# Projections split in two f32r terms: one 512-column matmul for the high weights, one of 256 for the low weights, and the two halves of the bank summed on VectorE

## The chip, the cores and the metric

One Trainium2 chip, one of its NeuronCores. The metric is the device time of one launch in microseconds, as a median over runs. One launch computes three layers of a small transformer-like stack for 256 tokens of width 2048.

## What is computed

The reference runs three layers one after the other in fp32. In outline (`@` is a matrix product over 2048 features unless said otherwise):

```
# layer A: modulated norm, sparse attention and a pooled branch, then experts
ada  = silu(c) @ w_ada + b_ada                      # six vectors of 2048
h    = rmsnorm(x) * (1 + sc1) + sh1
q, k, v, qi, ki, wi, p = split(h @ w_in)
mix  = concat(attention_topk(q, k, v, qi, ki, wi), pool(p))
x    = x + gt1 * (mix @ w_out)
x    = x + gt2 * experts(rmsnorm(x) * (1 + sc2) + sh2)   # top 2 of 32, SwiGLU
# layer B: gated linear recurrence and sliding-window attention
z    = rmsnorm(x) @ l0_w_in                         # lx, lg, bq, bk, bv, bs
x    = x + concat(rg_lru(lx) * silu(lg), window_attention(bq, bk, bv) * silu(bs)) @ l0_w_out
# layer C: latent attention and differential attention
z    = rmsnorm(x) @ l1_w_in                         # cq, ckv, kr, mg, dq, dk, dv, dg
q, kv = rmsnorm(cq) @ w_uq, rmsnorm(ckv) @ w_ukv
x    = x + concat(mla(q, kv, kr) * silu(mg), diff_attention(dq, dk, dv) * silu(dg)) @ l1_w_out
out  = rmsnorm(x)
```

## The kernel before

Activations lie transposed: 128 features on the partitions, 256 tokens along the free dimension, 16 chunks for 2048 features. A **projection** computes one chunk of 128 output features for all 256 tokens. Its weights are 16 blocks of 128 x 128, one for each chunk `kk` of input features, and arrive from HBM in two halves of eight blocks (512 KB each, `land`).

**Split operands.** TensorE's one-pass type f32r has fewer bits than fp32, so both operands are split. ScalarE copies a half of the weights to `WH` in f32r (step `hi`, L1370), and VectorE subtracts that from the original to get the rest, `WL` (step `lo`, L1654). The activations are split in the same way to `HH` and `HL` (steps `hh`/`hl`, `mh`/`ml`, `ch`/`cl`). Three matmuls for each block, all in one bank (`product`, L992), make the product: WH by HH, WL by HH, WH by HL. The weights are the stationary operand and 256 tokens the moving one, so each of the three loads 128 x 128 weights and streams 256 columns. 2552 blocks go this way. The value projections v, bv, dv and vm are **wide**: there the activations are stationary (L989).

**Stages.** Layer A's projections run with the streaming of `w_ada` between them (L1042), then come its attention jobs, the output projection `wo`, and a router. The experts follow (L1181 to L1235), a loop that streams 12 MB of weights for each tile of tokens. Then layer B (projections bk to lg, eight attention jobs, four groups of the recurrence, `wb`) and layer C (cq to mg, attention jobs `d`, the up-projections qn, qr, kn and vm with jobs `m`, then `wc`).

**Order of the work.** `order_a` and `order_bc` write out by hand, for each of PE, ACT and DVE, the list of steps that the engine runs in that order. A step waits for the steps it needs through one semaphore for each engine, and each engine also waits for its own step before. `Order.proj` adds a projection: the PE's `part` and `proj`, the evacuation `evac` on ACT, and a `load` (that is `hi` on ACT and `lo` on DVE) after each half, four halves ahead of their use. Later steps of older projections or jobs (norm, rotation, softmax) are added by `tick`.

**Banks.** Projections, the index products and every second gate product of the recurrence (`lgate`, L1148) take turns in two PSUM banks, `acc0` and `acc1`. In `bank_of` the PE waits until the step two before in that list has left its bank; before the change that is ACT's `evac`. For k, q, cq and ckv, `evac` makes a copy and a square. For wo, wb and wc it makes a copy `tm`, and DVE's step `res` adds that to the residual `X` (L1783).

## Time and profile before

| what | value |
|---|---|
| median of 3 runs | 2473.24 us (2471.9 to 2474.04) |
| span of the profiled execution | 2472.8 us |
| PE busy | 2121.0 us (86%) |
| DVE busy | 1214.8 us (49%) |
| ACT busy | 898.2 us (36%) |
| granted TensorE clock, mean | 0.938 of full speed |

The span is what the profile shows of one execution, from the first to the last instruction; the times of the runs are taken without the profiler. Names of tiles are the program's, L numbers are lines of the kernel before. PEld is TensorE's loading of weights, which overlaps its matmuls.

### The profile page before, as it was taken

The page shows a single profiled execution, that of the slowest core. Times are in us where ns is not written, and L with a number is a line of the kernel's source. Part 1 is how long each engine was busy: PE and PEld are TensorE (multiplying, and loading weights), DVE is VectorE, ACT ScalarE, POOL GpSimd, SP SyncE. Part 2 cuts the span into 40 slices and gives each one's busy share as a digit, 9 for nine tenths or more (in the row PEclk, how much of TensorE's full clock was granted, in tenths as well). Part 3 has the DMA queues.
Part 4 walks back from the last instruction along what each step waited for, and adds up shares of the span by engine and source line. Part 5 has one row for each costly group of instructions (what it writes and reads, how often), then busy time and mean ns, then how long its engine had stood idle before and what let it go on. Part 6 is the DMA issues. An engine that isn't in the chain of part 4 may idle for free.

```text
span 2472.8 us, 38254 instructions
## 1 busy us (share of the span) xinstructions
PE 2121.0 (86%) x14524; PEld 1408.1 (57%) x14524; DVE 1214.8 (49%) x2202; ACT 898.2 (36%) x1382; POOL 0.2 (0%) x4
## 2 busy tenths in 40 slices
PE   5699998986888788878887888799989799998987
PEld 1178776772222222222222222599889799997887
DVE  1254686445433333333333433646875554478555
ACT  1143344442211122211122121546865444465543
POOL 0000000000000000000000000000000000000000
PEclk7799999997999989999999999899999899998999
DMA  8979776766999999999999998365345355543442
GB/s 320 383 278 315 263 264 247 264 222 254 422 422 422 422 422 422 422 422 422 422 422 422 422 422 349 110 202 163 120 136 182 128 171 185 181 146 102 132 129 100
DMA packets 135046, 695.44 MB, mean 281 GB/s; under 512 B 14992, under 2 KB 15120, under 8 KB 85264
## 3 DMA queue, kind: packets, MB, share of 16 engines
q1 hardware_dynamic: 134928, 693.81, 73.5%
q8 instruction: 81, 1.33, 0.2%
q14 instruction: 37, 0.30, 0.0%
HBM read 691.66 MB, written 2.10 MB: 281 GB/s over the span
## 4 chain that ended last, share of the span: by engine, by line
PE 48%; DMA 37%; DVE 8%; ACT 4%; issue 2%; SPq 1%; DVEq 0%; ACTq 0%
DMA ring<-in_w 33%; PE acc L992 33%; DMA land<-in_stream_a 4%; PE acc L989 3%; PE psS L1218 3%; PE psO L1042 2%; DVE WL L1654 2%; ACT WH L1370 1%; PE psM L1073 1%; SPq L872 1%; DVE HL L1664 0%; ACT SB L1440 0%; PE psT L938 0%; PE psM L1206 0%; PE acc L1108 0%
## 5 line engine op out<-in xcount | busy, mean ns | idle before, releaser
L992 PE MATMUL acc<-HH,WH 128*128 128x256 f32 x2552 | 752.5, 295 | 47.4 <-DVE HL L1664 15.7
L992 PE MATMUL acc<-HH,WL 128*128 128x256 f32 x2552 | 728.9, 286 | 0.0
L992 PE MATMUL acc<-HL,WH 128*128 128x256 f32 x2552 | 728.5, 285 | 0.0
L1654 DVE TENSOR_TENSOR WL<-land,WH 128x1024 fp32r<-128x1024 f32 (+1 forms) x350 | 425.7, 1216 | 423.8 <-ACT WH L1370 419.7
L992 PEld LDWEIGHTS acc<-HH,WH 128*128 128x128 f32 x2552 | 495.9, 194 | 92.1 <-issue 16.2
L992 PEld LDWEIGHTS acc<-HH,WL 128*128 128x128 f32 x2552 | 497.0, 195 | 3.3 <-issue 2.2
L992 PEld LDWEIGHTS acc<-HL,WH 128*128 128x128 f32 x2552 | 496.4, 195 | 0.0
L1370 ACT ACTIVATE WH<-land 128x1024 fp32r<-128x1024 f32 (+1 forms) x350 | 367.9, 1051 | 252.9 <-PE acc L992 199.2
L1218 PE MATMUL psS<-ring,low 128*32 128x512 f32 x2048 | 282.8, 666 | 148.2 <-DMA ring<-in_w 126.2
L1218 PEld LDWEIGHTS psS<-ring,low 128*32 128x32 f32 x2048 | 53.8, 113 | 340.3 <-DMA ring<-in_w 251.7
L2037 DVE TENSOR_REDUCE SB<-psT 128x128 f32<-128x512 f32 x32 | 22.1, 692 | 389.5 <-PE psT L1228 389.5
L1206 PE MATMUL psM<-low 128*128 128x512 f32 x264 | 146.1, 635 | 23.3 <-DVE low L2028 21.2
L1518 ACT ACTIVATE low<-psO 128x512 f32<-128x512 f32 x32 | 19.1, 597 | 340.5 <-PE psO L1235 340.5
L1042 PE MATMUL psO<-land,high_a 128*32 128x512 f32 x672 | 103.8, 698 | 39.7 <-DMA land<-in_stream_a 37.5
L1206 PE MATMUL acc<-low 128*128 128x512 f32 x264 | 135.7, 596 | 0.0
L1512 ACT ACTIVATE low<-psS 128x512 f32<-128x512 f32 x64 | 38.2, 597 | 226.3 <-PE psS L1218 225.9
L1235 PE MATMUL psO<-ring,SB 128*32 128x512 f32 x1024 | 116.5, 595 | 0.0
L2028 DVE TENSOR_TENSOR low<-psM,low 128x512 f32<-128x512 f32 x132 | 91.1, 690 | 44.4 <-PE psM L1206 44.3
L2049 DVE TENSOR_SCALAR low<-low,cst 128x256 f32<-128x256 f32 x128 | 36.5, 349 | 140.3 <-ACT low L1522 140.3
L2028 DVE TENSOR_TENSOR low<-acc,low 128x512 f32<-128x512 f32 x132 | 90.9, 689 | 17.4 <-PE acc L1206 17.4
L1206 PEld LDWEIGHTS psM<-low 128*128 128x128 f32 x264 | 39.7, 189 | 100.8 <-DVE low L2028 98.2
L1181 PE MATMUL acc<-low,SB 128*32 128x512 f32 x528 | 82.7, 757 | 15.4 <-DVE SB L2006 15.4
(326 smaller groups left out, 1998.4 us busy)
## 6 DMA issues: line engine op xcount, KB each, us to landing
ring<-in_w SPq DMA_DIRECT2D x384, 1024.0 KB, 24.1
land<-in_stream_a SPq DMA_DIRECT2D x284, 512.0 KB, 7.3
land<-in_stream_bc SPq DMA_DIRECT2D x246, 512.0 KB, 4.0
land<-in_stream_bc SPq DMA_DIRECT2D x12, 384.0 KB, 3.3
X<-in_xT SPq DMA_DIRECT2D x1, 2048.0 KB, 16.3
out<-low SPq DMA_DIRECT2D x4, 512.0 KB, 2.7
cst<-in_const SPq DMA_DIRECT2D x1, 1538.0 KB, 12.4
low<-in_w_pool SPq DMA_DIRECT2D x1, 1024.0 KB, 5.2
```

The costliest lines, as they stand in the source:

```text
L989: mm = pe.matmul(bank[:, S * tt:S * tt + S], h[:, rows[kk], P * tt:P * tt + P], w[:, kk, :], start=(z == 0 and i == 0 and tt == 0), stop=s ...
L992: mm = pe.matmul(bank[:, 0:S], w[:, kk, :], h[:, rows[kk], :], start=(z == 0 and i == 0), stop=stop)
L1042: mm = pe.matmul(bank[CAP * c:CAP * c + CAP, :], cB[:, 4 * q + c, :], w[c // 2][:, c % 2, :], start=(q == 0), stop=(q == 3), tile_position ...
L1181: mm = pe.matmul(bG[CAP * n:CAP * n + CAP, :], SG[:, tt, :], H2[:, tt, 512 * n:512 * n + 512], start=(tt == 0), stop=(tt == NT - 1), tile_ ...
L1206: pe.matmul(ybank[m % 2], OE[:, P * c:P * c + P], SJ[:, 2 * half:2 * half + 2, :], start=True, stop=True).then_inc(moe["y_full"], 1)
L1218: mm = pe.matmul(bH[s // 4][CAP * c:CAP * c + CAP, :], XG[:, k % 4, k // 4, :], ring[:, s, 512 * c:512 * c + 512], start=(s % 4 == 0), sto ...
L1235: mm = pe.matmul(bW2[CAP * c:CAP * c + CAP, :], AT[:, s - 8, :], ring[:, s, 512 * c:512 * c + 512], start=(s == 8), stop=(s == 11), tile_p ...
L1370: ins = act.activation(WH[:, q % PARTS, 0:n], land[k][:, p % LAND[k], 0:n], ACT.Copy)
L1512: act.activation(HS[:, b, :], bankS[b], ACT.Copy).then_inc(moe["h_copied"], 1)
L1654: ins = dve.tensor_tensor(WL[:, q % PARTS, 0:n], land[k][:, p % LAND[k], 0:n], WH[:, q % PARTS, 0:n].bitcast(F32), ALU.subtract)
L2028: dve.tensor_tensor(y, src, y, ALU.add).then_inc(moe["y_added"], 1)
L2049: ins = dve.tensor_scalar(SJ[:, c, :], ST, K("group", c, 1), None, ALU.mult)
```

## The change

For projections that are not wide, WH by HH and WH by HL become one matmul of 512 columns. For that, HH and HL are the two halves of one tensor `HHL`; the first half of the bank takes WH by HH, the second WH by HL, and WL by HH is added to the first half as before. The two halves of the bank then have to be summed: a new DVE step `sum` adds the second half to what ACT's `evac` has copied of the first, and `bank_of` waits for that step. For wo, wb and wc there is no ACT copy any more: DVE's `res` adds each half of the bank to X, one after the other. The squares of k, q, cq and ckv become an ACT step of their own, `square`, which waits for `sum` and reads SBUF.

```diff
+SUMMED = ("k", "q", "qi", "ki", "wi", "p", "wo", "bk", "bq", "bs", "lx", "lg", "wb", "cq", "ckv", "kr", "dk", "dq", "dg", "mg",
+          "qn", "qr", "kn", "wc")
+RESIDUAL = ("wo", "wb", "wc")
...
         self.acc.append(("proj", x))
-        self.add("act", "evac", x)
+        if x[0] not in RESIDUAL:
+            self.add("act", "evac", x)
+            if x[0] in SUMMED:
+                self.add("dve", "sum", x)
+        if x[0] in ("k", "q", "cq", "ckv"):
+            self.add("act", "square", x)
...
-        HH = inside("HH", [P, KD, S], F32R, 8 * PARTS)
-        HL = inside("HL", [P, KD, S], F32R, 8 * PARTS + KD)
+        HHL = inside("HHL", [P, 2, KD, S], F32R, 8 * PARTS)
+        HH, HL = HHL[:, 0, :, :], HHL[:, 1, :, :]
...
-                terms = [(a, b, c, kk) for kk in range(len(rows)) for a, b, c in ((wh, HH, 0), (wl, HH, 1), (wh, HL, 2))]
+                terms = [(a, b, c, kk) for kk in range(len(rows)) for a, b, c in
+                         (((wh, HH, 0), (wl, HH, 1), (wh, HL, 2)) if wide else ((wh, HHL, 0), (wl, HH, 1)))]
...
+                        elif term == 0:
+                            mm = pe.matmul(bank.rearrange("p (a s) -> p a s", a=2), w[:, kk, :], HHL[:, :, rows[kk], :],
+                                           start=(z == 0 and i == 0), stop=False)
                         else:
-                            mm = pe.matmul(bank[:, 0:S], w[:, kk, :], h[:, rows[kk], :], start=(z == 0 and i == 0), stop=stop)
+                            mm = pe.matmul(bank[:, 0:S], w[:, kk, :], h[:, rows[kk], :], start=False, stop=stop)
...
-                        needs(k, "act", o, "evac", prev[1] if prev[0] == "proj" else prev)
-                    return acc[n % 2]
+                        if prev[0] == "proj":
+                            needs(k, evac_of(prev[1])[0], o, *evac_of(prev[1])[1:])
+                        else:
+                            needs(k, "act", o, "evac", prev)
+                    return acc[n % 2][:, :]
...
+                def add_other(x):
+
+                    other = acc[o.acc.index(("proj", x)) % 2][:, S:2 * S]
+                    needs("act", "evac", x)
...
+                    return dve.tensor_tensor(z, other, z, ALU.add)
...
-                            needs("act", "evac", step[1])
-                            tm = W((aTM if k == 0 else dTM) + n % 2)[:, 0, :]
-                            ins = dve.tensor_tensor(X[:, n, :], X[:, n, :], tm, ALU.add)
+                            needs("pe", "proj", step[1])
+                            bank, x = acc[o.acc.index(("proj", step[1])) % 2], X[:, n, :]
+                            for h in range(2):
+                                a = bank[:, S * h:S * h + S]
+                                if name == "wo":
+                                    ins = dve.scalar_tensor_tensor(out=x, in0=a, scalar=gt1[:, n:n + 1], in1=x, op0=ALU.mult, op1=ALU.add)
+                                else:
+                                    ins = dve.tensor_tensor(x, a, x, ALU.add)
+                                if h == 0:
+                                    then(ins)
```

**PE, layer B, around a gate product.** The end of a projection, an attention job's products (L946, L910), the two gate products (L1148) and the start of the next projection. Before:

```order
4109 L992 MATMUL acc<-HH,WL 128x256
4110 L992 MATMUL acc<-HL,WH 128x256
4111 L946 MATMUL psO<-PTS,low 128x512 [waits dve_done1,act_done1]
4112 L910 MATMUL psS<-low 128x2x128 [waits dve_done1]
4116 L1148 MATMUL acc<-low 128x256 [waits act_done1,dve_done1]
4117 L1148 MATMUL acc<-low 128x256
4118 L992 MATMUL acc<-HH,WH 128x256 [waits dve_done1,act_done1]
4119 L992 MATMUL acc<-HH,WL 128x256
4120 L992 MATMUL acc<-HL,WH 128x256
```

The same place in the changed kernel:

```order
2906 L1010 MATMUL acc<-HHL,WH 128x512
2907 L1013 MATMUL acc<-HHL,WL 128x256
2908 L963 MATMUL psO<-PTS,low 128x512 [waits dve_done1,act_done1]
2909 L927 MATMUL psS<-low 128x2x128 [waits dve_done1]
2913 L1172 MATMUL acc<-low 128x256 [waits dve_done1]
2914 L1172 MATMUL acc<-low 128x256
2915 L1010 MATMUL acc<-HHL,WH 128x512 [waits dve_done1]
2916 L1013 MATMUL acc<-HHL,WL 128x256
```

Three matmuls for a block have become two, and the first matmul of the next projection no longer waits for ACT but for DVE alone.

**DVE, at the same place.** `low<-psO` is a job's output, `SB<-psS` its softmax, `high_bc` and `low<-high_bc` the recurrence, `WL` the low parts of the weights. Before:

```order
690 L1654 TENSOR_TENSOR WL<-land_54,WH 128x1024 [waits act_done1,dve_done1] x2
691 L1942 TENSOR_TENSOR high_bc<-high_bc 128x256 [waits act_done1,dve_done1]
692 L1943 SCALAR_TENSOR_TENSOR low<-high_bc 128x256 [waits dve_link]
695 L1654 TENSOR_TENSOR WL<-land_54,WH 128x1024 [waits act_done1,dve_done1] x2
696 L1620 TENSOR_TENSOR low<-psO,low 64x2x128 [waits pe_done1,dve_done1]
```

Now:

```order
811 L1697 TENSOR_TENSOR WL<-land_53,WH 128x1024 [waits act_done1,dve_done1]
812 L1666 TENSOR_TENSOR low<-acc,low 128x256 [waits act_done1,dve_done1]
813 L1697 TENSOR_TENSOR WL<-land_53,WH 128x1024 [waits act_done1,dve_done1]
814 L1990 TENSOR_TENSOR high_bc<-high_bc 128x256 [waits act_done1,dve_done1]
815 L1991 SCALAR_TENSOR_TENSOR low<-high_bc 128x256 [waits dve_link]
818 L1697 TENSOR_TENSOR WL<-land_53,WH 128x1024 [waits act_done1,dve_done1]
819 L1666 TENSOR_TENSOR low<-acc,low 128x256 [waits act_done1,dve_done1]
820 L1697 TENSOR_TENSOR WL<-land_53,WH 128x1024 [waits act_done1,dve_done1]
821 L1644 TENSOR_TENSOR low<-psO,low 64x2x128 [waits pe_done1,dve_done1]
```

Between the two `lo` steps that stood in a pair there is now the sum of a projection (L1666), behind whatever DVE has still to do.

## Rows read from the trace of the kernel before

**Rows 1.** The page: busy time, share of the span, instructions.

```profile
PE 2121.0 (86%) x14524; PEld 1408.1 (57%) x14524; DVE 1214.8 (49%) x2202; ACT 898.2 (36%) x1382; POOL 0.2 (0%) x4
```

**Rows 2.** The page: the chain that ended last, by engine and by line.

```profile
PE 48%; DMA 37%; DVE 8%; ACT 4%; issue 2%; SPq 1%; DVEq 0%; ACTq 0%
DMA ring<-in_w 33%; PE acc L992 33%; DMA land<-in_stream_a 4%; PE acc L989 3%; PE psS L1218 3%; PE psO L1042 2%; DVE WL L1654 2%; ACT WH L1370 1%; PE psM L1073 1%; SPq L872 1%; DVE HL L1664 0%; ACT SB L1440 0%; PE psT L938 0%; PE psM L1206 0%; PE acc L1108 0%
```

**Rows 3.** Stretches of the span: engines' busy us, granted clock, DMA share, GB/s.

```profile
core 0: us, PE busy (x) PEld busy (x) DVE busy (x) ACT busy (x) POOL busy (x), PEclk, DMA share, GB/s
186.00:248.00 62.00, 62.00 (x488) 50.88 (x487) 28.33 (x43) 20.35 (x25) 0.00 (x0) 1.00 0.91 316
2030.00:2090.00 60.00, 60.00 (x503) 60.00 (x502) 25.65 (x22) 26.08 (x31) 0.00 (x0) 1.00 0.57 181
1720.00:1850.00 130.00, 121.66 (x876) 111.00 (x876) 106.77 (x183) 98.70 (x160) 0.00 (x0) 0.99 0.40 131
```

**Rows 4.** The chain by line in 310 to 440, 1720 to 1850, 2190 to 2370 us.

```profile
by line: PE acc L992 25.3%; PE acc L1108 8.0%; DVE WL L1654 7.6%; DMA land<-in_stream_a 5.4%; PE psM L1042 5.4%; DVE high_a L1744 5.3%; issue 4.8%; DVE small L1743 4.6%; PE psS L905 2.9%; DVE low L1705 2.7%; ACT WH L1370 2.5%; PE psT L938 1
by line: PE acc L992 48.9%; DVE WL L1654 6.7%; issue 5.6%; ACT WH L1370 4.1%; PE psS L910 3.3%; PE psO L946 3.3%; ACT SB L1440 2.4%; PE psT L938 2.4%; PE psM L1148 2.0%; PE acc L1148 2.0%; DVE SB L1607 2.0%; ACT L1440 2.0%; DVE HL L1676 1.9
by line: PE acc L992 39.7%; ACT WH L1370 6.3%; DVE WL L1654 5.2%; ACT SB L1440 4.9%; PE acc L989 4.8%; PE psO L951 4.5%; issue 4.2%; PE psS L915 3.3%; ACT HH L1396 2.4%; PE psT L938 2.2%; ACT low L1401 2.1%; DVE high_bc L1966 1.9%; PE psM L
```

**Rows 5.** Chain pieces: start us, length us, what.

```profile
1717.47 5.75 PE acc L992 x48
1723.22 1.72 PE psO L946 x4
1734.13 0.44 PE psT L938 x4
2314.26 0.22 PE psS L922 x2
```

**Rows 6.** Timeline of PE at the upper clock: start us, length us, instruction.

```profile
2020.14 0.28 PE L992 MATMUL acc<-HH,WL 128*128 128x256 f32 x1
2020.14 0.19 PEld L992 LDWEIGHTS acc<-HL,WH 128*128 128x128 f32 x1
2020.26 0.28 PE L992 MATMUL acc<-HL,WH 128*128 128x256 f32 x1
```

**Rows 7.** Timeline of PE at the lower clock, from 427.34 us.

```profile
427.69 0.42 PE L992 MATMUL acc<-HH,WL 128*128 128x256 f32 x1
...
429.83 0.41 PE L992 MATMUL acc<-HL,WH 128*128 128x256 f32 x1
```

**Rows 8.** Groups: shapes and count, busy us, mean ns of one, idle before and what ended it.

```profile
L938 PEld LDWEIGHTS psT<-cst,SB 128*128 128x128 f32 x120 | 13.5, 143 | 15.2 <-DVE SB L1607 6.7 <-DVE SB L1602 6.0 <-issue 1.7
L922 PEld LDWEIGHTS psS<-low 128*128 128x128 f32 x32 | 5.3, 191 | 0.3
L1716 DVE TENSOR_TENSOR low<-psT,cst 128x256 f32<-128x256 f32 x19 | 8.1, 425 | 1.5 <-PE psT L1092 0.9
L1783 DVE TENSOR_TENSOR X<-X,high_bc 128x256 f32<-128x256 f32 x32 | 13.6, 426 | 28.6 <-ACT high_bc L1311 28.5
L1311 ACT ACTIVATE high_bc<-acc 128x256 f32<-128x256 f32 x32 | 12.4, 387 | 60.2 <-PE acc L992 57.3 <-issue 3.0
```

**Rows 9.** Timeline around a gate product at 1775 us.

```profile
1775.94 1.03 PE L1148 MATMUL acc<-low 128*128 128x256 f32 x4
1776.09 0.38 ACT L1329 ACTIVATE low<-acc 128x256 f32<-128x256 f32 x1
1776.62 0.47 PE L992 MATMUL acc<-HH,WH 128*128 128x256 f32 x1
1777.17 0.69 DVE L1943 TENSOR_TENSOR_SCAN low<-high_bc 128x256 f32<-128x256 f32 x1
1777.90 2.49 DVE L1654 TENSOR_TENSOR WL<-land,WH 128x1024 fp32r<-128x1024 f32 x2
```

**Rows 10.** Timeline around the next gate product, at 1799 us.

```profile
1799.05 0.38 ACT L1329 ACTIVATE low<-acc 128x256 f32<-128x256 f32 x1 [1.46 <-PE acc L992]
1800.76 0.47 PE L992 MATMUL acc<-HH,WH 128*128 128x256 f32 x1
1802.49 2.48 DVE L1654 TENSOR_TENSOR WL<-land,WH 128x1024 fp32r<-128x1024 f32 x2
```

**Rows 11.** Timeline of DVE in the up-projections of layer C.

```profile
2301.35 3.35 DVE L1966 RECIPROCAL high_bc<-high_bc 128x512 f32<-128x512 f32 x1
```

More of the change, by code:

```diff
@@ L124, in constants, with evac_of @@
     return t
+SUMMED = ("k", "q", "qi", "ki", "wi", "p", "wo", "bk", "bq", "bs", "lx", "lg", "wb", "cq", "ckv", "kr", "dk", "dq", "dg", "mg",
+          "qn", "qr", "kn", "wc")
+RESIDUAL = ("wo", "wb", "wc")
+def evac_of(x):
+    if x[0] in RESIDUAL:
+        return "dve", "res", x
+    return ("dve", "sum", x) if x[0] in SUMMED else ("act", "evac", x)
 LAGS = {"a": (1, 2, 3, 4), "b": (1, 2, 3, 4), "d": (1, 2, 3, 4), "m": (1, 3, 5, 6)}
@@ L917, in attention @@
                     else:
-                        needs(k, "act", o, "evac", ("kn", 4 * j[1] + 3))
+                        needs(k, "dve", o, "sum", ("kn", 4 * j[1] + 3))
                         needs(k, "dve", o, "rot", ("qr", 3))
@@ L1054, in run @@
                         misc_free(step)
-                        needs(k, "act", o, "evac", ("wi", 0))
+                        needs(k, "dve", o, "sum", ("wi", 0))
                         for tt in range(NT):
@@ L1071, in run @@
                         else:
-                            needs(k, "act", o, "sq" if x[0] == "moe" else "evac", x)
+                            needs(k, "act", o, "sq" if x[0] == "moe" else "square", x)
                         mm = pe.matmul(psM[:, 0:S], ones[:, :], sq, start=(x in FIRST_SS), stop=(x[1] == LAST.get(x[0], KD - 1)))
@@ L1076, in run @@
                         misc_free(step)
-                        needs(k, "act", o, "evac", x)
+                        needs(k, "act", o, "square", x)
                         mm = pe.matmul(psM[:, 0:S], ones[:, :], W(aSQ + nr.index(x) % 2)[:, 0, :], start=True, stop=True)
@@ L1090, in run @@
                         else:
-                            needs(k, "act", o, "evac", x)
+                            needs(k, "dve", o, "sum", x)
                         mm = pe.matmul((psM if n is None else bankT[0])[:, 0:S], K(rot_of(x)), rot_chunk(x), start=True, stop=True)
@@ L1275, in evac @@
                     if name in ("k", "q"):
-                        i = nr.index(x)
-                        if i >= 2:
-                            needs("pe", "nrm", nr[i - 2])
-                        act.activation(rot_chunk(x), a, ACT.Copy)
-                        return act.activation(W(aSQ + i % 2)[:, 0, :], a, ACT.Square)
+                        return act.activation(rot_chunk(x), a, ACT.Copy)
                     if name in ("qi", "ki", "qr"):
@@ L1341, in evac @@
                     if name in ("cq", "ckv"):
-                        if n >= 2:
-                            needs("pe", "ss", (name, n - 2))
-                        act.activation(W((cCQ if name == "cq" else cCKV) + n)[:, 0, :], a, ACT.Copy)
-                        return act.activation(W(dSQ + n % 2)[:, 0, :], a, ACT.Square)
+                        return act.activation(W((cCQ if name == "cq" else cCKV) + n)[:, 0, :], a, ACT.Copy)
                     if name in ("dk", "dq"):
@@ L1357, in run @@
                         ins = evac(step[1])
+                    elif what == "square":
+                        x = step[1]
+                        name, n = x
+                        needs("dve", "sum", x)
+                        if name in ("k", "q"):
+                            i = nr.index(x)
+                            if i >= 2:
+                                needs("pe", "nrm", nr[i - 2])
+                            ins = act.activation(W(aSQ + i % 2)[:, 0, :], rot_chunk(x), ACT.Square)
+                        else:
+                            if n >= 2:
+                                needs("pe", "ss", (name, n - 2))
+                            ins = act.activation(W(dSQ + n % 2)[:, 0, :], W((cCQ if name == "cq" else cCKV) + n)[:, 0, :], ACT.Square)
                     elif what == "silu_c":
@@ L1399, in run @@
                         _, name, n, size = step
+                        needs("dve", "sum", (name, n + size - 1))
                         z = W(MIX + n + (8 if name in ("bs", "dg") else 0), size)
@@ L1625, in attention_out @@
                     return dve.tensor_tensor(mix, psO[:, :, :], mix, ALU.mult)
+                def add_other(x):
+                    other = acc[o.acc.index(("proj", x)) % 2][:, S:2 * S]
+                    needs("act", "evac", x)
+                    name, n = x
+                    if name == "bk":
+                        z = W(bK + 2 * n, 2)
+                        dve.tensor_tensor(z[0:64, 0, :], other[0:64, :], z[0:64, 0, :], ALU.add)
+                        return dve.tensor_tensor(z[64:128, 1, :], other[64:128, :], z[64:128, 1, :], ALU.add)
+                    at = {"wi": aWI, "p": aPR, "bq": bQ, "lg": MIX, "mg": MIX, "bs": MIX + 8, "dg": MIX + 8, "cq": cCQ, "ckv": cCKV,
+                          "dk": cDK, "dq": cDQ, "qn": cQN, "kn": cKN}
+                    if name in ("k", "q", "qi", "ki", "qr", "kr"):
+                        z = rot_chunk(x)
+                    else:
+                        z = W(bLX + n % 2 if name == "lx" else at[name] + n)[:, 0, :]
+                    return dve.tensor_tensor(z, other, z, ALU.add)
                 def rms(n, width):
@@ L1634, in run @@
                         dve.wait_ge(done[k]["dve"], count)
-                    if what == "setup":
+                    if what == "sum":
+                        ins = add_other(step[1])
+                    elif what == "setup":
                         dve.memset(ones[:, :], 1.0)
@@ L1751, in run @@
                         p = W(aPR + 2 * g, 2)
-                        needs("act", "evac", ("p", 2 * g + 1))
                         a, b = W(aPS, 2), W(aPS + 2, 2)
@@ L1915, in run @@
                         n = step[1]
-                        needs("act", "evac", ("lx", n))
                         x, y = W(bLX + n % 2)[:, 0, :], W(bY + n)[:, 0, :]
@@ L1949, in run @@
                         p = step[1]
-                        needs("act", "evac", ("dk", 2 * p + 1))
                         if p:
```

8 lines of the change are left out of this document (1 added, 7 removed).

## The prediction

> **What bounds the kernel now.** Read the busy shares first: TensorE (PE) is busy 86% of the span, VectorE (DVE) 49%, ScalarE (ACT) 36% [rows 1]. A share says nothing of single stages, so the chain that ended last comes next [rows 2]: a third of it is the DMA of expert weights, which this change does not touch, and another third, 33% of 2472.8 us or 816 us, is line L992, the three-matmul product that it rewrites. DVE has 8% of the chain, ACT 4%. So the product is on the path for most of its time, and outside the experts a faster product shortens the kernel if the next limit is not close behind.
>
> How close it is shows in the stretches [rows 3]. At 2030 to 2090 us PE is busy without a gap, and DVE only 25.65 of 60 us: there a gain on PE is a gain. At 1720 to 1850 us DVE is busy 106.77 and ACT 98.70 of 130 us. The chain of that stretch, and of 310 to 440 us and 2190 to 2370 us, changes often between PE, DVE and ACT, with L992 at 48.9%, 25.3% and 39.7% [rows 4]. There DVE work is on the path too. DMA has room: its share is 0.91 at 316 GB/s in one of the densest stretches of layer A, and 0.57 in layer C [rows 3].
>
> **What a matmul of the product costs.** In a steady run 48 of them take 5.75 us [rows 5], 119.8 ns each; the timeline shows the same spacing of 0.12 us, and each load of weights starting with the matmul before it [rows 6]. The clock there is the upper level of 2.4 GHz (granted 1.00, [rows 3]), so 256 columns at one a cycle are 106.7 ns, and 13.1 ns are something else. What? Three rows help. At the lower level, 1.2 GHz, ten matmuls take 2.14 us [rows 7], 214 ns each against 213.3 for 256 columns: the rest is hidden. The fp32 products, two cycles a column in each record, take 430 ns for 512 columns and 110 ns for 128 [rows 5], against 426.7 and 106.7: a rest of 3 ns, and this holds for a short load of 143 ns (L938) and a full one of 191 ns (L922) alike [rows 8]. So a full load alone fits into about 110 ns. The 13 ns appear only where columns stream at one a cycle with a load beside them.
>
> **The change on PE.** For each block it removes one load of weights and one matmul, and makes another twice as wide. Now: 3 x 119.8 = 359.4 ns. After: one of 256, taken at 119.8 ns, and one of 512, which no row shows at one column a cycle. Its bounds: from below 213.3 + 3 = 216 ns, if the rest belongs to a load that hinders the stream (the load covers less than half of 512 columns); from above 2 x 119.8 = 239.6 ns, if the stream itself runs at 0.468 ns a column. Between them lies a fixed cost for each matmul, 213.3 + 13.1 = 226.4 ns. I take 222 ns, midway between 216 and 226.4 with the fp32 rows in mind: they speak for a small fixed part. That is 341.6 ns a block, a saving of **17.8 ns**; the fixed cost alone would give 13.2 ns.
>
> The Trainium skill (TensorE: Matmul & The Clock Gate, Back-to-back issue gap) gives for an isolated matmul at the upper clock N/2.4 + 2.5 ns: 109.2 ns for 256 columns and 215.8 for 512. By that rule a block would go from 327.5 to 325.0 ns and the change would save 2.5 ns. The trace shows 119.8 instead of 109.2 for this product, so the rule does not describe it, and the sum goes by the rows.
>
> **How many blocks count.** 816 us of chain are 2270 blocks of 359.4 ns, of 2552. In the three mixed stretches L992 has 0.253 x 130 + 0.489 x 130 + 0.397 x 180 = 168 us of chain [rows 4], or 467 blocks. A second chain on DVE and ACT runs close beside there, so I count half of them. 2270 - 234 = 2036 blocks by 17.8 ns are **36.2 us gained**.
>
> **The change on DVE and ACT.** 125 projections get a `sum`: a 256-column DVE operation with one input in PSUM, as L1716, 425 ns [rows 8]; 127 instructions, since bk needs two, 54 us. Each residual step becomes two such operations instead of one of 426 ns on SBUF (L1783): 48 more, 20 us. ACT loses the 48 copies of wo, wb and wc, 387 ns each (L1311), 19 us. In the PE-bound stretches DVE's idle time hides all of this: a projection there takes 5.5 us, its two `lo` steps 2.5, its sum 0.43. In the mixed stretches there are some 55 projections (about 10, 17 and 28); 55 x 0.44 = 24 us of new DVE work, and half of it falls where DVE is on the path: **12 us lost**.
>
> **The wait that the change adds.** The PE may write a bank again only after DVE's `sum`, where ACT's copy was enough. Between two projections on end there are 5.5 us for that, and nothing waits. But a gate product takes the other bank, so the next projection needs at once the bank of the last one. At 1776 us ACT had copied it by 1776.47 and the PE went on at 1776.62, while the DVE pair of `lo` steps that now has the sum between them ran from 1777.90 to 1780.39 [rows 9]: the sum would end at 1779.6, 3.0 us after the PE's start. At 1799 us the same comes to 1804.2 against 1800.76, 3.4 us [rows 10]. The first two gate products come earlier or find DVE free. The up-projections kn are short (four blocks, under 1.5 us), and one can stand behind the reciprocal of 3.35 us [rows 11]. Together 6.4 + up to 3.4; the stretches that follow are partly DVE's anyway, so I take **8 us**. ACT's new `square` waits for DVE in the middle of its queue, with `hi` behind it: half a microsecond for 20 projections, which the four halves split ahead cover, and at the stage ends, where the last residual chain stays as long (a PSUM add for an ACT copy), about **1 us**. The wide projections keep their form.
>
> **Sum**: -36.2 + 12 + 8 + 1 = -15 us, on the profiled span of 2472.8 us: 2458 us. The median of the runs, 2473.24, lies 0.4 us from that span, so this serves as the forecast for the median too. About 0.2%, 4.9 us, is what a measurement of this kernel can tell from no change.
>
> **Rivals.** *The load is the whole rest.* Then 512 columns cost 216 ns and the narrow matmul, with a load beside fewer streaming columns, about 113: 329 ns a block, 30 ns saved, 61 us over 2036 blocks; less 21 us, 2433 us. For it: the fp32 rows with their rest of 3 ns, and the lower clock without one. Against it: the narrow matmul keeps a full load beside it.
>
> *The stream is the limit.* If one-pass f32r data cannot be read faster than 0.468 ns a column, two halves in one matmul cost 239.6 ns, PE gains nothing, and the sums and bank waits remain: +21 us at most, some of them hidden in PE's slack, 2490 us. For it: a full-rate stream of 4-byte elements is the one thing that sets this product apart from the fp32 rows. Against it: nothing in the trace needs it. It decides from 229 ns for the wide matmul on: below a saving of 21 us / 2036 = 10.3 ns a block the kernel is not faster. The skill's rule above would end here too: 2.5 ns a block are 5 us, 2489 us.
>
> *DVE becomes the bound.* If in the mixed stretches each of the 55 projections pays its sum and a wait behind half a `lo` pair, 0.44 + 0.6 us, 57 us stand in place of 20; with the gain of 36 us, 2494 us. For it: DVE is busy 82% of 1720 to 1850 us. Against it: for most of layers A and C it has over half its time free.
>
> **Chances.** The forecast with its near cases (a saving of 13 to 20 ns a block, 2450 to 2467 us) 0.45; the load 0.25; the stream 0.20; DVE 0.10. Nearly all of the first two is faster by over 0.2%, the upper edge of the forecast is not; in the last two a part may end within 0.2%: faster 0.64, same 0.11, slower 0.25. The range leaves out the outer part of each rival: 2428 to 2488 us.
>
> **What would show it.** Right: wide matmuls spaced 216 to 227 ns at full clock, blocks of about 342 ns, PE busy through 2030 to 2090 us with fewer microseconds for each projection, DVE near 1290 us, and PE waits on the new DVE sum of some 3 us at two gate products. Wrong: wide matmuls at 240 ns; PE waits on sums at every projection of a mixed stretch; or waits on DMA in layer A, which the 0.91 leaves little room for.

## The result, and the profile after

The changed kernel is slower, by less than one per cent. Its median is 2490.52 us (2486.77 to 2491.46, 4 runs) against 2473.64 (2471.9 to 2476.71, 4 runs) of the kernel before: a ratio of 1.007, 95% interval 1.0056 to 1.0084, or 14 to 21 us. The profiled execution has a span of 2488.6 us against 2472.8.

The first section and the chain of the page of the changed kernel answer to [rows 1] and [rows 2]. L1010 is the 512-column matmul, L1013 the one of 256, L1007 the value projections that kept their form:

```profile
PE 2111.5 (85%) x11972; PEld 1272.3 (51%) x11972; DVE 1290.2 (52%) x2377; ACT 881.5 (35%) x1334; POOL 0.2 (0%) x4
PE 45%; DMA 37%; DVE 10%; ACT 5%; issue 2%; SPq 1%; DVEq 0%; ACTq 0%
```

TensorE issues 2552 matmuls and loads fewer, and the product has 31% of the chain (L1010 21%, L1013 10%) after 33%. VectorE has 75.4 us more work (74 in the forecast), and its share of the chain went from 8 to 10%.

The timeline of TensorE in a dense piece of layer C (start us, length us, instruction) stands beside [rows 6]:

```profile
2050.12 0.40 PE L1010 MATMUL acc<-HHL,WH 128*128 128x512 f32 x1
2050.35 0.28 PE L1013 MATMUL acc<-HHL,WL 128*128 128x256 f32 x1
2050.47 0.40 PE L1010 MATMUL acc<-HHL,WH 128*128 128x512 f32 x1
2050.71 0.28 PE L1013 MATMUL acc<-HHL,WL 128*128 128x256 f32 x1
2050.83 0.40 PE L1010 MATMUL acc<-HHL,WH 128*128 128x512 f32 x1
```

A block, wide and narrow, takes 0.35 to 0.36 us. In 2030 to 2090 us, where TensorE never stops, the starts of the narrow matmuls lie 346, 356 and 358 ns apart in turn, 353.4 ns in the mean of 170; in the kernel before all 167 blocks of that stretch take 360.0 ns. The change saves **6.6 ns** a block where the forecast had 17.8. Over the undisturbed blocks of 1850 to 2090 us the saving is 7.5 ns: a wide matmul takes 235.7 ns from start to start (572 of them) and the narrow one 116.6 (573), 352.3 together, against 359.9.

Stretches of the span, as in [rows 3]:

```profile
2030.00:2090.00 60.00, 60.00 (x342) 52.05 (x341) 31.85 (x36) 26.34 (x32) 0.00 (x0) 1.00 0.56 187
1720.00:1850.00 130.00, 110.34 (x548) 88.75 (x546) 105.91 (x188) 91.65 (x144) 0.00 (x0) 0.93 0.36 118
```

In the first TensorE is busy without a gap, as it was. In the second it is busy 110.34 us of 130 after 121.66, and its granted clock is 0.93 after 0.99: it waits more, and part of its work runs slower. For what it waits, the view of the waits says (what waits, for what, us in total, times, longest), for 1742 to 1845 us and then for 2290 to 2385 us:

```profile
PE acc L1010 <- DVE low L1666: 10.6, 3, 5.2
...
PE acc L1010 <- DVE low L1666: 5.1, 2, 4.2
```

L1666 is the new `sum`. In the kernel before the longest waits of these stretches were for the split activations, and no wait of the product on a copy out of the bank was among the listed ones:

```profile
PE acc L992 <- DVE HL L1676: 5.9, 2, 3.5
...
PE acc L992 <- DVE HL L1676: 3.8, 2, 2.2
```

A third new wait stands in 226 to 348 us, where the q projections run; there TensorE is held by ScalarE's copy of the index product (L1317, high_a), and ScalarE by the sum, before the square (L1376):

```profile
PE acc L1010 <- ACT high_a L1317: 5.2, 5, 1.4
ACT high_a L1376 <- DVE low L1666: 4.3, 4, 1.7
```

The program has the same 354 halves of projections in both kernels, so the start of each can be set against the start of the same one before. The changed kernel stands 1.1 us behind at the end of the experts (1591 us), gains down to 1.4 us ahead by 1742 us, loses 15.1 us from there to 1842 us, gains 4.1 by 2298 us, loses 8.9 by 2382 us. This reading is used for all kernels below.

The three stretches that lose are shown here over the same work in both kernels, first of the kernel before, then of the changed one, with the columns of [rows 3]:

```profile
226.60:348.10 121.50, 114.21 (x819) 89.04 (x818) 81.35 (x147) 46.37 (x73) 0.00 (x0) 0.99 0.78 273
1742.00:1842.10 100.10, 91.76 (x663) 83.80 (x661) 85.20 (x147) 79.26 (x122) 0.00 (x0) 0.98 0.39 127
2298.00:2382.30 84.30, 75.47 (x586) 72.88 (x585) 49.83 (x65) 46.95 (x85) 0.00 (x0) 0.98 0.35 113
...
221.80:349.60 127.80, 115.90 (x626) 79.87 (x625) 85.90 (x159) 47.37 (x73) 0.00 (x0) 0.96 0.74 260
1740.70:1855.90 115.20, 95.54 (x469) 77.56 (x468) 90.47 (x159) 78.88 (x121) 0.00 (x0) 0.91 0.34 112
2307.70:2400.90 93.20, 79.57 (x468) 69.97 (x467) 56.50 (x82) 46.20 (x83) 0.00 (x0) 0.91 0.30 102
```

They take 30.3 us more. TensorE stands idle for 20.7 of these us, and is busy for 9.6 us more although it has less to do, because more of its work falls into time at the lower of its two clock levels (1.2 and 2.4 GHz): a share of 0.5 is the lower level, so 121.5 x 0.01, 100.1 x 0.02 and 84.3 x 0.02, taken twice, give some 10 us of such time before, and the shares below them some 48 us now. The 501 blocks of these stretches should have saved 3.3 us, so the lower clock costs about 13 us, an estimate from these rows.

### The profile page after: what moved, and what is told of

Same layout as the page of the kernel before. It is cut to its first block, busy times and chain, and to the rows that moved or that the text cites. A ratio compares the mean times of both kernels' runs of the same rounds, so it can differ in the third digit from the quotient of the medians.

```text
span 2488.6 us, 33366 instructions
## 1 busy us (share of the span) xinstructions
PE 2111.5 (85%) x11972; PEld 1272.3 (51%) x11972; DVE 1290.2 (52%) x2377; ACT 881.5 (35%) x1334; POOL 0.2 (0%) x4
## 4 chain that ended last, share of the span: by engine, by line
PE 45%; DMA 37%; DVE 10%; ACT 5%; issue 2%; SPq 1%; DVEq 0%; ACTq 0%
DMA ring<-in_w 33%; PE acc L1010 21%; PE acc L1013 10%; DMA land<-in_stream_a 4%; PE acc L1007 3%; PE psS L1242 3%; DVE WL L1697 2%; PE psO L1066 2%; ACT WH L1393 2%; SPq L889 1%; PE psM L1097 1%; ACT SB L1464 1%; DVE HHL L1707 0%; PE psM L1230 0%; PE psO L968 0%
## 5 line engine op out<-in xcount | busy, mean ns | idle before, releaser
L1010 PE MATMUL acc<-HHL,WH 128*128 128x512 f32 x2552 | 952.1, 414 | 66.4 <-DVE HHL L1707 16.5
L1013 PE MATMUL acc<-HHL,WL 128*128 128x256 f32 x2552 | 727.3, 285 | 0.0
L1010 PEld LDWEIGHTS acc<-HHL,WH 128*128 128x128 f32 x2552 | 492.2, 193 | 230.2 <-DVE HHL L1707 22.6
L1013 PEld LDWEIGHTS acc<-HHL,WL 128*128 128x128 f32 x2552 | 495.8, 194 | 3.4 <-issue 2.4
L1666 DVE TENSOR_TENSOR low<-acc,low 128x256 f32<-128x256 f32 x115 | 48.8, 424 | 68.8 <-ACT low L1357 13.7
```

Source lines behind the costliest of these rows:

```text
L1010: mm = pe.matmul(bank.rearrange("p (a s) -> p a s", a=2), w[:, kk, :], HHL[:, :, rows[kk], :], start=(z == 0 and i == 0), stop=False)
L1013: mm = pe.matmul(bank[:, 0:S], w[:, kk, :], h[:, rows[kk], :], start=False, stop=stop)
```

## The experiments

Each ratio below is to runs of the kernel before that were taken together with the experiment; their medians lie between 2471.1 and 2474.2 us. The expectations are in us without such a correction, so a miss of one or two us says nothing.

### The two halves of the change, one at a time

`e1_three_mm` keeps sums, waits and both halves of the bank and takes the wide matmul away:

```
-  (((wh, HH, 0), (wl, HH, 1), (wh, HL, 2)) if wide else ((wh, HHL, 0), (wl, HH, 1)))
+  ((wh, HH, 0), (wl, HH, 1), (wh, HL, 2))
...
+  half = S if term == 2 else 0
+  mm = pe.matmul(bank[:, half:half + S], w[:, kk, :], h[:, rows[kk], :], ...)
```

> The sums, their waits and the use of both halves of the bank stay; the 512-column matmul is split back into two of 256, high by high into the first half and high by low into the second. Against the kernel before this carries the sums and waits alone, against the changed kernel it lacks the wide matmul alone. Theory A (the two parts add up: the wide matmul saves some 5 ns a block over 2036 to 2552 blocks, 10 to 13 us, and the sums with their waits cost 27 to 30): 2500 to 2503 us. Rival B (the sums cost only where PE comes to a bank too early, so that a slower PE hardly waits): 2485 to 2492, about the changed kernel's time. Rival C (the wide matmul itself costs time, the sums are nearly free): 2473 to 2478.

Measured: 2508.21 us, ratio to before 1.0154 (1.0136 to 1.0171): sums and waits cost 34 to 42 us. That is above theory A's 2500 to 2503 us, and further from both rivals.

`e2_no_sums` is the kernel before with the wide matmul alone; its output lacks the product of high weights and low activations:

```
-  HH = inside("HH", [P, KD, S], F32R, 8 * PARTS)
-  HL = inside("HL", [P, KD, S], F32R, 8 * PARTS + KD)
+  HHL = inside("HHL", [P, 2, KD, S], F32R, 8 * PARTS)
...
+  mm = pe.matmul(bank[:, :].rearrange("p (a s) -> p a s", a=2), w[:, kk, :], HHL[:, :, rows[kk], :], ...)
```

> The kernel before with the wide matmul alone: the second half of the bank (high weights by low activations) is computed and never added, so this product is left out of the output; steps, waits and copies are those of the kernel before. Theory A (a block goes from 359 to some 354 ns, nothing else): 2460 to 2464 us. Rival D (the forecast's step was right in itself, 341.6 ns a block, and its gain was eaten by waits): 2435 to 2445. Rival C (the wide matmul costs time): over 2476.

Measured: 2456.05 us, ratio 0.9938 (0.992 to 0.9956): 11 to 20 us faster, somewhat more than theory A's 2460 to 2464 us. The interval holds the 2270 blocks of the chain by 6.6 ns, 15 us, and excludes the 36 us of the forecast. The blocks take what they take in the changed kernel, 353.3 ns in 2030 to 2090 us. So the two parts go the ways that theory A says, though both are larger: +38 and -15 give +23, +17 was measured, and the two ratios' intervals, each some 4 us to either side, cover the difference. Rivals B, C and D are out.

### What a matmul takes, by its columns

`e3_columns` takes the kernel before and replaces the matmuls of seven of the eight k projections of layer C; these products are left out.

```
+  elif name == "dk" and n == 3:
+      mm = pe.matmul(bank[:, 0:2 * S], w[:, kk, :], hf[:, S * rows[kk]:S * rows[kk] + 2 * S], ...)
+  elif name == "dk" and n == 5:
+      mm = pe.matmul(bank[:, :].rearrange("p (a s) -> p a s", a=2), w[:, kk, :], HHL[:, :, rows[kk], :], ...)
...
```

> A probe: the kernel before, in which the eight k projections of the differential attention (stage C) issue other matmuls in place of their own, so their product is left out; the times of consecutive matmuls of one line are read. By turns: bf16 zeros of 256 and of 512 columns, float32r of 512 columns in one run and in two runs of 256, of 384 columns, of 128 columns, and 256 columns with 32 stationary columns instead of 128. Theory A (the stream of float32r columns is the limit, 0.46 to 0.468 ns a column at the upper clock, and the load hides behind it): 512 columns 236 to 240 ns in one run as in two, 384 columns 177 to 180, 256 with 32 stationary columns still 118 to 120; 128 columns at or above 60. Rival G (the pattern of two runs slows the wide matmul): 512 in one run clearly under 236 ns. Rival H (the load of the 128 stationary columns is part of the 119.8 ns): with 32 stationary columns well under 119. bf16 at 256 columns says whether the limit is that of float32r (bf16 then under 119.8) or of the columns themselves (the same).

The timeline of TensorE in this kernel; L1000 and L998 are bf16, L1014 float32r with 512 columns in two runs, L1006 with 384:

```profile
2018.62 1.24 PE L1000 MATMUL acc<-zero 128*128 128x512 bf16 x5
...
2009.82 0.93 PE L998 MATMUL acc<-zero 128*128 128x256 bf16 x7
...
2036.21 0.39 PE L1014 MATMUL acc<-HHL,WL 128*128 128x512 f32 x1
2036.43 0.39 PE L1014 MATMUL acc<-HHL,WH 128*128 128x512 f32 x1
2036.66 0.39 PE L1014 MATMUL acc<-HHL,WL 128*128 128x512 f32 x1
2036.89 0.39 PE L1014 MATMUL acc<-HHL,WH 128*128 128x512 f32 x1
...
2046.43 0.34 PE L1006 MATMUL acc<-HHL,WL 128*128 128x384 f32 x1
2046.61 0.35 PE L1006 MATMUL acc<-HHL,WH 128*128 128x384 f32 x1
```

The usual spacing of the 30 or so starts of each form, in the records' whole nanoseconds:

| form | ns from start to start | at one column a cycle | rest |
|---|---|---|---|
| bf16, 256 columns | 109 | 106.7 | 2 |
| bf16, 512 | 216 | 213.3 | 3 |
| float32r, 128 | 109 to 115 | 53.3 | (floor) |
| float32r, 256 | 120 | 106.7 | 13 |
| float32r, 256, 32 stationary columns | 117 to 118 | 106.7 | 11 |
| float32r, 384 | 173 to 174 | 160 | 13 |
| float32r, 512 in one run, or in two | 226 to 227 | 213.3 | 13 |

Theory A's reason falls: the stream is not slow, 512 columns behind 512 take 226.5 ns, not 237. Float32r pays a fixed 13 ns for each matmul, whatever its columns, from 256 to 512. With 32 stationary columns the load takes 108 ns in place of 188, and only 2 of the 13 ns go, so the load is not the rest either (rival H). Its 98 ns of load beside bf16 are near that, and bf16 keeps a rest of 2 to 3 ns. Two runs cost nothing over one (rival G). The bf16 rows use zeros and the same weights each time, so a dependence on the values is not excluded.

The Trainium skill (TensorE: Matmul & The Clock Gate, Back-to-back issue gap) has N/2.4 + 2.5 ns for an isolated matmul: 109.2 and 215.8. For bf16 the trace agrees, 109 and 216; for float32r the matmul takes 10.6 ns more at 256 columns and at 512.

But then a block should take 226.5 + 119.8 = 346.3 ns, and it takes 353.4. Seven nanoseconds go where wide and narrow ones alternate.

### Why the pair takes 353 ns

`e8_pairs` issues sequences of both widths in the same eight projections (left out again), in the changed kernel:

```
+  seq = {0: [(f, kk) for kk in range(8) for f in ("one", "low")], ...
+         4: [(f, kk) for f in ("two", "low") for kk in range(8)], ...
+         7: [(f, kk + g) for kk in range(0, 8, 2) for f in ("two", "low") for g in (0, 1)]}[n]
```

> A probe: the changed kernel, in which the eight k projections of the differential attention issue other sequences of matmuls, so their product is left out; read are the times of consecutive starts. By turns (each for 16 chunks): 512 columns in one run then 256; 512 in two runs then 256 (as in the changed kernel); 512 then 256 into the second half; 512 then 384; eight of 512 then eight of 256; 512, 256, 256; 512 then 256 with 32 stationary columns each; two of 512 then two of 256. Theory I (the change of width costs 8 ns): pairs 354 ns in the first, second and third; 354 + 53.5 with 384; grouped 346; 512, 256, 256 about 474; two and two about 350 a pair. Rival J: grouped 354 too. With 32 stationary columns under 350 if the load is what the alternation disturbs, 350 to 354 if not.

In every alternating pair the wide matmul takes 232, 240 and 236 ns in turn and the narrow one behind it 118, 120 and 114, 353.3 together in the mean: in one run or two, and with the narrow one into the other half. With 32 stationary columns the means are 231.5 and 117.0, 348.5. With a 384-column partner the wide one takes 231 to 233 and the other 175, 406. With two narrow ones behind each wide one the three settle at 465 to 469 ns, where 226.5 + 2 x 119.8 would be 466.1 and theory I had 474; two and two take 349 ns a pair. In eight and eight the first wide ones behind the narrow ones take 229 to 236 ns and the last ones 226 to 227, the narrow ones 120, 347 to 349 a pair. So a wide matmul costs some 229 to 240 ns when it stands close behind a narrow one and 226.5 when several of its kind stand before it. Rival J, which had 354 for the grouped order too, is out; theory I, with 346 there and 350 for two and two, is near, but the change of width as such costs nothing: the last wide one of a row and the first narrow one behind it take 227 and 113.

`e5_grouped` puts this into the changed kernel:

```
-  (((wh, HH, 0), (wl, HH, 1), (wh, HL, 2)) if wide else ((wh, HHL, 0), (wl, HH, 1)))]
+  ((wh, HH, 0), (wl, HH, 1), (wh, HL, 2))] if wide else [
+      (a, b, c, kk) for a, b, c in ((wh, HHL, 0), (wl, HH, 1)) for kk in range(len(rows))]
```

> The changed kernel with the order of the terms turned: in each weight half first the eight 512-column matmuls, then the eight of 256, in place of one and one. The probe before gave 226.5 ns for a 512-column matmul behind another and 119.8 for 256 behind 256, 346.3 together, where the changed kernel's pairs take 354. Theory I (it is the alternation of the two widths that costs 8 ns a pair): 8 ns x 2036 to 2552 pairs off, 2470 to 2475 us. Rival J (the pair takes 354 ns because accumulating into the whole bank and its half is slow in any order, or because of the loads): 2488 to 2492.

Measured: 2490.65 us, 1.0073 (1.0061 to 1.0085): nothing gained, the time that rival J gave. The spacings do not bear J out. The mean spacings of undisturbed matmuls in 1850 to 2090 us are 230.7 ns between wide ones and 118.9 between narrow ones, some 349 ns a block with the changes of width, against 352.3. The rows of eight begin at 233 to 236 ns and end at 227: they are too short to bring 226.5 throughout. Three ns on 2270 blocks would still be 7 us, and the measured time, which can hide some 4, does not show them; why stays open. What the chip does in the 7 ns stays open too. The pattern of the moving operand and the half of the bank change nothing, a shorter load takes 4 to 5 ns off a pair (348.5, just under the 350 that was to tell), as much as in the table above for two matmuls; what remains is the width of the matmuls before.

### Where the sums cost

`e4_act_frees` lets ScalarE copy both halves out and free the bank, VectorE adds from SBUF:

```
 def evac_of(x):
...
-    return ("dve", "sum", x) if x[0] in SUMMED else ("act", "evac", x)
+    return "act", "evac", x
...
+  act.activation(other[:, i % 2, :], b, ACT.Copy)
```

> The changed kernel, but ScalarE copies both halves out of the bank (the second into one of two 1 KB buffers) and alone frees it, so that TensorE waits for no VectorE step there; VectorE adds from SBUF, the same number of additions as in the changed kernel; ScalarE has some 115 copies of about 0.4 us more. Theory A with the bank waits as the loss: the waits on the sums at the three gate products and at the up-projections are gone, 2463 to 2475 us. Rival E (the loss is VectorE's own added work, which delays the split of the weights, or the squares that now come after the sum): 2484 to 2492. Rival F (ScalarE becomes late instead): over 2492.

Measured: 2485.04 us, 1.0058 (1.0044 to 1.0072). That lies in the range of rival E (VectorE's own work, or the squares behind the sums), not in theory A's: by the ratios it is some 3 us less than the changed kernel, and the intervals overlap. ScalarE has some 115 copies more here, so this kernel alone does not separate the causes; its stretches, below, do better.

`e7_idle_adds` adds the load on VectorE, without the residuals' part, to the kernel before, and no one waits for it:

```
+  if what == "sum":
+      needs("act", "evac", step[1])
+      ins = dve.tensor_tensor(other[:, 0, :], other[:, 1, :], other[:, 1, :], ALU.add)
```

> The kernel before with 112 or so additions of 256 columns on VectorE, SBUF to SBUF, at the places where the changed kernel has its sums (after the same ScalarE copy), of a buffer that nothing reads: matmuls, bank waits, squares and copies are those of the kernel before; what it does not have is anybody waiting for a sum. Theory A (bank waits at the gate products, squares behind the sums in the q stretch): 2472 to 2479 us. Rival E (VectorE's own added work holds up the split of the weights and the softmax): 2485 to 2505.

Measured: 2478.35 us, 1.0027 (1.0017 to 1.0037): 4 to 9 us. The median is inside theory A's range; with the slower runs of the kernel before in the first measurement, 2473.64 us, the ratio gives 2480, just above it. Both are below rival E's: VectorE's own work is the smaller part.

Where each kernel loses (+) and gains (-) against before, in us, from the starts of the same half of a projection:

| stretch of the kernel before | e2 | e1 | changed | e4 | e7 |
|---|---|---|---|---|---|
| 0 to 226 | -3.2 | -4.1 | -4.8 | -3.4 | -3.6 |
| 226 to 348, q projections and index | +0.6 | +7.7 | +6.3 | +7.9 | +0.5 |
| 348 to 1742 | -4.4 | +0.6 | -2.8 | -4.6 | -3.4 |
| 1742 to 1842, recurrence and its gates | +2.4 | +15.8 | +15.1 | +4.7 | +2.8 |
| 1842 to 2298 | -5.7 | +3.1 | -4.1 | -0.1 | -0.4 |
| 2298 to 2382, up-projections | +0.7 | +7.3 | +8.9 | +5.3 | +2.5 |
| 2382 to 2454 | -2.7 | 0.0 | -2.6 | -1.3 | 0.0 |

(The -3.6 of e7 in the first row and its -3.4 in the third, where it can gain nothing, show what the start, attention and expert stages of one execution vary by; all five kernels lead in the first row, so part of that is the profiled execution of the kernel before.) Three stretches hold the loss, and two different waits. At the gates the bank wait is the cause: e4 takes 10 of the 15 us away. The timeline of the changed kernel there, DVE's queue from the gate product on:

```profile
1750.49 1.03 PE L1172 MATMUL acc<-low 128*128 128x256 f32 x4
1751.04 0.69 DVE L1599 SCALAR_TENSOR_TENSOR SB<-psS,cst 128x512 f32<-128x512 f32 x1
1751.77 0.69 DVE L1602 TENSOR_REDUCE small<-SB 128x4 f32<-128x512 f32 x1
...
1753.41 1.52 DVE L1969 SCALAR_TENSOR_TENSOR low<-low,col 128x255 f32<-128x255 f32 x3
1754.97 1.23 DVE L1697 TENSOR_TENSOR WL<-land,WH 128x1024 fp32r<-128x1024 f32 x1
1756.23 0.42 DVE L1666 TENSOR_TENSOR low<-acc,low 128x256 f32<-128x256 f32 x1
1756.71 0.80 PE L1010 MATMUL acc<-HHL,WH 128*128 128x512 f32 x1 [5.19 <-DVE low L1666]
```

The gate product took the one bank, the next projection needs the other, and the 0.42 us that free it stand behind a softmax head, a convolution and a split of weights: TensorE waits 5.19 us. This is the second of the four gate products that take a bank, at 1726, 1750, 1782 and 1806 us. The first is followed by no such wait, the third by 1.03 us, the fourth by 4.41 us behind another softmax head; and in the up-projections a sum stands behind the reciprocal:

```profile
1784.04 0.50 PE L1010 MATMUL acc<-HHL,WH 128*128 128x512 f32 x1 [1.03 <-DVE low L1666]
...
1811.94 0.58 PE L1010 MATMUL acc<-HHL,WH 128*128 128x512 f32 x1 [4.41 <-DVE low L1666]
...
2310.92 3.35 DVE L2013 RECIPROCAL high_bc<-high_bc 128x512 f32<-128x512 f32 x1
2316.30 0.50 PE L1010 MATMUL acc<-HHL,WH 128*128 128x512 f32 x1 [4.16 <-DVE low L1666]
```

The wait costs more than its length. Behind the 1.03 us the granted clock stays at 1.00. Behind the 5.19 us TensorE's granted clock is 0.51 from 1754 to 1761 us, and the blocks there take 0.64 us in place of 0.35:

```profile
1754.00:1761.00 7.00, 4.29 (x13) 3.72 (x14) 6.65 (x12) 5.00 (x15) 0.00 (x0) 0.51 0.41 141
...
1757.51 0.63 PE L1010 MATMUL acc<-HHL,WH 128*128 128x512 f32 x1
1757.94 0.41 PE L1013 MATMUL acc<-HHL,WL 128*128 128x256 f32 x1
1758.15 0.63 PE L1010 MATMUL acc<-HHL,WH 128*128 128x512 f32 x1
```

In the q stretch e4 keeps the changed kernel's loss, so it is not the bank, and e7 has none, so it is not VectorE's load. What both e1 and e4 share with the changed kernel is the square behind the sum. `e9_square_behind` moves it on ScalarE's queue:

```
-  if x[0] in ("k", "q", "cq", "ckv"):
+  if x[0] in ("k", "cq", "ckv"):
       self.add("act", "square", x)
...
       for _ in range(2): ... o.add("act", "evac", ("idx", i)); o.add("dve", "idx", i)
+      o.add("act", "square", x)
```

> The changed kernel with one thing moved: the square of each of the eight q projections, which waits for VectorE's sum, stands on ScalarE's queue behind the copies of the next two index products instead of before them; it still precedes the reduction that needs it. Theory L (in the q stretch ScalarE is held at the square until the sum is made, and the index copies and their banks behind it come late): the 6 us lost between 226 and 348 us shrink to 1 to 2, 2484 to 2487 us, and TensorE's waits for the index copy go from 5.2 us back to the 0 of the page of before. Rival M (the stretch loses on VectorE's own chain of sum, rotation and index additions): 2488 to 2493 with the stretch as before this run.

Measured: 2483.59 us, 1.0038 (1.0023 to 1.0053), just below theory L's 2484 to 2487 us; rival M is out. The 226 to 348 us stretch goes from +6.3 to -1.1 us, the others stay (+15.0 and +7.5), and of TensorE's wait for the index copy, 5.2 us in the changed kernel and 0.7 in the one before, this is left:

```profile
PE acc L1011 <- ACT high_a L1318: 0.4, 1, 0.4
```

`e11_gates` puts lx and lg alone back to three matmuls:

```
-  SUMMED = (..., "bs", "lx", "lg", "wb", ...)
+  SUMMED = (..., "bs", "wb", ...)
```

> The changed kernel with lx and lg alone (16 projections between 1742 and 1842 us) back to three 256-column matmuls without a sum. Theory A for the gate products (their bank waits for a sum that stands behind the recurrence's and the softmax's operations on VectorE): the 15 us that the trace of the changed kernel loses there against before go but for 1 to 2, 2476 to 2479 us; the waits of 5.2 us on the sum at TensorE are gone. Rival N (the load on VectorE around it, with the sums of bs and the residual, holds the stretch up anyway): 2484 to 2490.

Measured: 2479.37 us, 1.002 (1.0011 to 1.0029): 1742 to 1842 us goes from +15.1 to -1.8, and the waits on the sum there are gone. So is the lower clock, which was granted 0.91 over this work in the changed kernel; 1746.2 to 1844.6 us is the same work here:

```profile
1746.20:1844.60 98.40, 89.94 (x630) 80.61 (x629) 85.62 (x148) 78.94 (x121) 0.00 (x0) 1.00 0.38 129
```

The q stretch (+8.2) and the up-projections (+8.4) stay. The median lies at theory A's upper edge; rival N is out. The edit takes sum and wide matmul away together; that it is the wait and not VectorE's load, e4 and e7 say.

### Versions that keep the sums only where they are free

`e6_selective` has neither sum nor wide matmul in any of the three stretches:

```
+  SUMMED = ("p", "wo", "bk", "bq", "bs", "wb", "cq", "ckv", "kr", "dk", "dq", "dg", "mg", "wc")
...
+  (((wh, HHL, 0), (wl, HH, 1)) if name in SUMMED else ((wh, HH, 0), (wl, HH, 1), (wh, HL, 2)))
```

> The changed kernel, but 36 of its 153 full projections and all 20 small ones (k, q, qi, ki, wi; the recurrence's lx and lg; the up-projections qn, qr, kn) go back to three 256-column matmuls, one copy by ScalarE and no sum. These are the three stretches in which the traces put the loss (+8, +16 and +7 us in the kernel of three matmuls with sums). 117 projections of 16 blocks keep the wide matmul. Theory A with the loss in those stretches: they cost nothing now, and 1872 blocks gain 5.4 ns, 10 us: 2460 to 2466 us. Rival K (sums cost elsewhere too, once VectorE is not held up before): 2470 to 2480.

Measured: 2464.35 us, 0.9968 (0.9957 to 0.9979): 5 to 11 us faster than before, in theory A's range; rival K is out. Its 1872 wide blocks by 6.6 ns would be 12 us, a little above that interval. `e10_q_wide` adds the q stretch with the squares behind:

```
+  SUMMED = ("k", "q", "qi", "ki", "wi", "p", "wo", "bk", "bq", "bs", "wb", "cq", "ckv", "kr", "dk", "dq", "dg", "mg", "wc")
...
+      o.add("act", "square", x)
```

> The selective kernel of the second set, but the q stretch (k, q, qi, ki, wi; 20 projections) too has the wide matmul and the sums, with the q squares behind the index copies. Three 256-column matmuls are left at lx, lg, qn, qr and kn. Theory L: the q stretch gains 20 projections x 16 blocks x 5.4 ns = 1.7 us and loses 1 to 2: 2461 to 2466 us, no difference from the selective kernel that can be told. Rival M: 5 to 6 us above it, 2468 to 2471.

Measured: 2459.33 us, 0.994 (0.9925 to 0.9954): 11 to 19 us faster than before, and as fast as the wide matmul without any sum. Stretches: -1.0, +1.4 and -0.3 us where the changed kernel has +6.3, +15.1 and +8.9. It is the fastest of the kernels that compute every product. It beats e6 by more than the 1.7 us expected: the two intervals do not overlap. Where the difference comes from is not shown, for the profiled execution is the slowest of its five (2465.88 us, the others 2457.68 to 2460.0), with a span of 2464.1 us against e6's 2462.1.

The wide matmul with both halves accumulated into the same 256 columns, which would need no sum at all, was not tried.

## Why the prediction was wrong

The sign and the range were wrong: 2458 us, 2428 to 2488, against 2490.5. The rival "the stream is the limit" gave 2490, and that was luck: it had no gain and a loss of 21 us where the runs have a gain of some 15 and a loss of some 33, and its reason is refuted by the probe.

- *What bounds the kernel.* Right. Where TensorE is busy without a gap the changed kernel gains steadily: 4.1 us from 1842 to 2298 us. In the three mixed stretches it loses.
- *Bounds for the wide matmul, 216 to 239.6 ns.* They held: 235.7. The value taken, 222, did not. The fp32 rows, which "speak for a small fixed part", misled here: the 13 ns are a fixed cost of a float32r matmul, 226.5 ns for 512 columns in a long row, as the middle case of the prediction had it. And what a wide matmul takes more behind narrow ones was in no row before. The first step that failed is this term: **17.8 ns a block, 6.6 measured**. The prediction itself had the kernel no faster below 10.3 ns.
- *Blocks on the chain.* 2036 by 6.6 ns are 13 us, 2270 are 15; the wide matmul alone gained 11 to 20. The count was not the fault: -36.2 should have been about -13 to -15.
- *DVE's added work, +12 us.* e7 has 4 to 9 us for the sums outside the residuals. The order of size was right.
- *The bank wait, +8 us.* The mechanism was right, the size too small. The waits come to 10.6 us at three gate products and 5.1 at the up-projections, 15.7 in all. The two gate products that were priced from rows, at 3.0 and 3.4 us, came to 1.0 and 4.4, together near the forecast, and the sum behind the reciprocal waited 4.2 us where up to 3.4 was expected. "The first two gate products come earlier or find DVE free" failed for the second: there TensorE waits longest, 5.2 us, because DVE's queue was read for the later two only, and a softmax head and a convolution stood in front.
- *Squares and boundaries, "about 1 us".* The second step that failed. The four halves split ahead do cover the weights; what they do not cover is the index copy behind the square and its bank. It cost 7.4 us in the traces, and 8 us between the ratios of the changed kernel and e9 (1.007 and 1.0038): a wait on the queue of an engine that is 35% busy.
- *The clock.* The prediction prices each wait by its length and puts nothing for what TensorE's clock does behind it. In the three stretches that is about 13 us, by the estimate above, and with the waits of a stretch it goes, as e11 shows. It is no cost beside the stretches' losses but a part of them.
- *Sum.* -15 as measured for the matmul, and +33 (changed kernel against e2, 1.007 / 0.9938 = 1.0133) for the rest where the forecast had +21, give the +17.
- *Rival "DVE becomes the bound".* Its price per projection was wrong, its direction right for the gates, where the bank wait made DVE's queue the path.

## What to carry to other kernels

A wider matmul saves only the fixed part of the one it absorbs; measure that part in the operand's type and in the order in which the widths will alternate, for rows of another type do not give it. When an operation is split between two engines, every step queued behind the new wait has to be read through, on each engine and at every place where banks are taken out of turn, and a cheap step (0.42 us) costs what stands ahead of it, and what the work behind the wait loses at a lower clock. Here the same change pays once the few projections around such places keep their old form, or the steps behind the wait are put in another order: 30 us of loss lay in three stretches that hold 36 of 153 full projections and the small ones.

## What the runs showed of the hardware

- A float32r matmul has a fixed 13 ns beyond one column a cycle at 256, 384 and 512 columns, where bf16 (of zeros) has 2 to 3 ns. With 32 stationary columns in place of 128, 11 ns remain. 128 columns take 109 to 115 ns, 30 of 31 times: below some width the spacing no longer falls.
- Two runs of 256 columns, 16 KB apart, read as fast as 512 on end: 226 to 227 ns both.
- A wide float32r matmul behind a narrow one takes 232 to 240 ns, in a cycle of three lengths, the narrow one 114 to 120; the cause is open.
- Behind TensorE's wait of 5.19 us the granted clock was 0.51 from 1754 to 1761 us, and a block took 0.64 us in place of 0.35. Over the 30.3 us that three stretches lost, some 10 us at the lower clock became 48.
